# A four-layer float32 block: two mask levels of its recurrence copied by ScalarE, two small steps given to GpSimd, and the conditioning chunks spread anew

## The reference, cut to what matters

```python
for l in range(DEPTH):
    mod = silu_c @ w_ada[l] + b_ada[l]
    sh_a, sc_a, g_a, sh_f, sc_f, g_f = jnp.split(mod[:, None, :], 6, axis=-1)
    hx = rmsnorm(x) * (1 + sc_a) + sh_a
    ux = hx @ w_in[l]
    ...                       # Fourier mixer, attention, recurrence (below)
    x = x + g_a * (jnp.concatenate([fx, ax, rx], axis=-1) @ w_out[l])
    x = x + g_f * swiglu(rmsnorm(x) * (1 + sc_f) + sh_f, w_gate[l], w_up[l], w_down[l])

def hg_gate(z, lb):           # per direction d, columns OFF_Z + 256 d of u
    k = (1.0 - lb) * jax.nn.sigmoid(-z)
    log_f = jnp.log(lb + (1.0 - lb) * jax.nn.sigmoid(z))
def step(s, inp):             # a chunk of tokens, forwards and backwards
    cum = jnp.cumsum(lf, axis=2)
    s_new = exp(last) * s + einsum('bhsd,bhse->bhde', kc * exp(last - cum), vc)
    o_inter = einsum('bhtd,bhde->bhte', qc * exp(cum), s)
    att = einsum('bhtd,bhsd,bhtsd->bhts', qc, kc, exp(masked cum_t - cum_s))
    return s_new, o_inter + einsum('bhts,bhse->bhte', att, vc)
```

## Time and profile before

| | us |
|---|---|
| median of 3 runs (2050.8 to 2056.23) | 2055.1 |
| the profiled execution | 2060.7 |
| its span | 2058.5 |
| PE busy (x12110) | 1798.2 (87%) |
| DVE busy | 1325.0 (64%) |
| ACT busy | 825.8 (40%) |
| POOL busy | 60.2 (3%) |
| mean granted PE clock | 0.911 |

### The profile page before, as it was taken

One profiled execution on the slowest core, in us unless ns is written; L12 is line 12 of the kernel. 1 busy time (PEld: TensorE's weight loads), 2 busy tenths in 40 slices (PEclk: granted clock), 3 DMA queues, 4 the chain that ended last, 5 costly groups with the idle time before them and its releaser, 6 DMA issues.

```text
span 2058.5 us, 30617 instructions
## 1 busy us (share of the span) xinstructions
PE 1798.2 (87%) x12110; PEld 1615.2 (78%) x12110; DVE 1325.0 (64%) x2468; ACT 825.8 (40%) x1593; POOL 60.2 (3%) x133
## 2 busy tenths in 40 slices
PE   4799878989999999897787999777799996879997
PEld 2689667978888888796577998675799976769996
DVE  1435868558877565587665888657478875474544
ACT  3433743142312232436524343356344434554432
POOL 0000022000000000000110000000000000000000
PEclk8899988889999999898578999988899999899999
DMA  9462011145546653332216898631489853314653
GB/s 283 129 205 64 25 47 38 31 134 164 179 159 205 184 179 109 92 105 65 70 34 180 264 273 272 203 97 27 144 241 273 278 201 112 104 42 138 183 179 126
DMA packets 359116, 300.32 MB, mean 146 GB/s; under 512 B 8048, under 2 KB 333408, under 8 KB 358720
## 3 DMA queue, kind: packets, MB, share of 16 engines
q1 hardware_dynamic: 357584, 294.22, 46.4%
q0 software_dynamic: 1392, 4.15, 0.9%
HBM read 297.30 MB, written 1.05 MB: 145 GB/s over the span
## 4 chain that ended last, share of the span: by engine, by line
PE 72%; DVE 12%; DMA 6%; issue 5%; ACT 5%; SPq 0%; DVEq 0%; ACTq 0%; POOLq 0%
PE bank L862 69%; PE bank L876 3%; ACT whigh L1391 2%; DMA raw<-in_w_down 1%; DVE wlow L1821 1%; DMA raw<-in_w_up 1%; DVE A L2243 1%; DMA raw<-in_ffn_w_out 1%; DVE A L1918 1%; DVE A L2120 1%; DVE HTL L1924 1%; DVE ACC L1837 1%; DMA A<-in_w_ada 1%; DMA AWH<-in_ada_w 1%; ACT A L1566 1%
## 5 line engine op out<-in xcount | busy, mean ns | idle before, releaser
L1821 DVE TENSOR_TENSOR wlow<-raw,whigh 128x2048 fp32r<-128x2048 f32 (+1 forms) x183 | 410.0, 2243 | 335.8 <-ACT whigh L1391 335.6
L1391 ACT ACTIVATE whigh<-raw 128x2048 fp32r<-128x2048 f32 (+1 forms) x183 | 343.2, 1877 | 553.7 <-PE bank L862 335.3
L862 PE MATMUL bank<-HTH,whigh 128*128 128x256 f32 (+1 forms) x1424 | 449.1, 315 | 12.5 <-DVE HTL L1924 12.5
L862 PE MATMUL bank<-HTH,wlow 128*128 128x256 f32 (+1 forms) x1424 | 444.0, 312 | 0.0
L862 PE MATMUL bank<-HTL,whigh 128*128 128x256 f32 (+1 forms) x1424 | 443.9, 312 | 0.0
L862 PE MATMUL bank<-whigh,HTH 128*128 128x256 f32 (+1 forms) x1008 | 296.8, 294 | 20.4 <-DVE HTL L1924 8.4
L862 PEld LDWEIGHTS bank<-HTH,whigh 128*128 128x128 f32 x1424 | 277.8, 195 | 26.1 <-issue 13.6
L862 PE MATMUL bank<-wlow,HTH 128*128 128x256 f32 (+1 forms) x1008 | 292.7, 290 | 0.0
L862 PE MATMUL bank<-whigh,HTL 128*128 128x256 f32 (+1 forms) x1008 | 292.3, 290 | 0.0
L862 PEld LDWEIGHTS bank<-HTH,wlow 128*128 128x128 f32 x1424 | 277.3, 195 | 13.6
L862 PEld LDWEIGHTS bank<-HTL,whigh 128*128 128x128 f32 x1424 | 277.8, 195 | 12.6
(11 more groups left out here) (207 smaller groups left out, 2191.0 us busy)
## 6 DMA issues: line engine op xcount, KB each, us to landing
raw<-in_ffn_w_in SPq DMA_DIRECT2D x88, 512.0 KB, 5.2
A<-in_ada_w SPq DMA_DIRECT2D x42, 1024.0 KB, 7.3
A<-in_w_ada SPq DMA_DIRECT2D x32, 1024.0 KB, 5.4
raw<-in_w_gate SPq DMA_DIRECT2D x44, 512.0 KB, 5.2
raw<-in_w_up SPq DMA_DIRECT2D x44, 512.0 KB, 6.3
raw<-in_ffn_w_out SPq DMA_DIRECT2D x20, 1024.0 KB, 5.0
raw<-in_w_in SPq DMA_DIRECT2D x18, 1024.0 KB, 6.2
raw<-in_w_down SPq DMA_DIRECT2D x18, 1024.0 KB, 6.7
```

The source lines that it names most:

```text
L862: return nc.tensor.matmul(out, lhsT, rhs, start=start, stop=stop, skip_group_check=True)
L1391: nc.scalar.activation(parts(loads[n])[0], raw_slot(loads[n]), ACT.Copy).then_inc(*made("split_high", loads[n]))
L1821: V.tensor_tensor(low, raw_slot(loads[n]), as_float(high), ALU.subtract).then_inc(*made("split_low", loads[n]))
```

## The change

1. **Conditioning respread** (`ada_plan`): 31 chunks beside the feed-forward of layer 0 (30 before), 10 in the recurrence of layer 1 (6), 17 beside the feed-forward of layer 1 (20), 18 beside that of layer 2 (20). The ten spots of the recurrence are two after step 0, one after each of steps 1, 2 and 3, two after step 4, one after each of 5, 6 and 7; before they were one after each of steps 0, 1, 2, 4, 5 and 6.
2. **ACT's order in the feed-forward**: `late` (the drain of `mod`) before `split`.
3. **Two levels copied as blocks**: the levels are weighed and multiplied in the order 4, 5, 6, 0, 1, 2, 3. Levels 6 and 5 are copied by ACT in three copies (64 partitions x 256, and twice 32 x 128); DVE masks 4, 0, 1, 2, 3 after those copies.
4. **The clamp** is done by POOL in place, for each of 4 tiles once (128 x 512), ahead of `gained`; `gate_in` is gone, and ACT's `gates_open` reads `U`.
5. **`QP`** is made by POOL (`query_decays`), one step later in POOL's order than the step's own pairs.

```diff
@@ ada_plan
-    give(feed_forward(0, 30))
-    give(scan(1, 6))
-    give(feed_forward(1, 20))
+    give(feed_forward(0, 31))
+    give(scan(1, 10))
+    give(feed_forward(1, 17))
     give(feed_forward(2, len(chunks)))
@@
+        LEVEL_ORDER = (4, 5, 6, 0, 1, 2, 3)
+        MASK_ORDER = (4, 0, 1, 2, 3)
+        def block_copies(d):
+            out = []
+            for j in (6, 5):
+                w = 1 << j
+                for b in range(P // (2 * w)):
+                    keys, queries = (2 * w * b + w * i for i in (1 - later(d), later(d)))
+                    out.append((j, slice(keys, keys + w), slice(queries, queries + w), slice(w * b, w * b + w)))
+            return out
+        def need_masked(eng, l, s, j):
+            eng.wait_ge(*upto("masked", l, s, 4 if j == ROUND_END[1] else MASK_ORDER[-1]))
+            eng.wait_ge(*upto("blocks_copied", l, s))
@@ gpsimd
+            def clamped(l):
+                for t in tiles_of(l, "mix"):
+                    ...
+                    z = U[:, t, OFF_Z:OFF_Z + 512]
+                    nc.gpsimd.tensor_scalar(z, z, LOWEST_GATE, None, ALU.max).then_inc(*made("clamped", l, t))
+            def query_decays(l, s, t, before):
+                for p in range(2):
+                    pool.wait_ge(*drained("e", l, s, p, 1))
+                pool.wait_ge(*drained("qt2", l, t))
+                if before:
+                    pool.wait_ge(*upto("read_out", l, s - 2))
+                nc.gpsimd.tensor_tensor(QP[:, s % 2], HW[s % 2][:, :, 7, :], qt2(l, t), ALU.mult) \
+                    .then_inc(*made("query_decays", l, s))
@@ own_pairs, ahead of the pairs of output step n
+                    if n:
+                        query_decays(l, outs[n - 1], scan_steps(l)[outs[n - 1]][1], n - 1 >= 2)
@@ tensor
-                    pe.wait_ge(*upto("masked", l, s, LEVELS - 1))
+                    need_masked(pe, l, s, ROUND_END[0])
+                    pe.wait_ge(*upto("query_decays", l, s))
-                        for j in range(LEVELS):
+                        for j in LEVEL_ORDER:
@@ scalar, recurrence
-                    act.wait_ge(*upto("gate_in", l, s))
-                    if l and n >= 2:
-                        act.wait_ge(*upto("gates", l, s - 2))
-                    nc.scalar.activation(HE[g], HS[g], ACT.Exp, scale=-1.0).then_inc(*made("gate_exp", l, s))
+                    act.wait_ge(*upto("clamped", l, t))
+                    if n >= 2:
+                        act.wait_ge(*(upto("gates", l, s - 2) if l else upto("gate_sum", l, s - 2)))
+                    z = U[:, t, OFF_Z + 256 * d:OFF_Z + 256 * d + 256]
+                    nc.scalar.activation(HE[g], z, ACT.Exp, scale=-1.0).then_inc(*made("gate_exp", l, s))
+                def copy_blocks(n):
+                    s, t, d, has_out = steps[n]
+                    act.wait_ge(*upto("product", "a", l, s, ROUND_END[1]))
+                    ...
+                    for j, keys, queries, at in block_copies(d):
+                        last = nc.scalar.activation(AS[keys, d, :, queries], PAIRS[1][keys, :, j % 4, at], ACT.Copy)
+                    last.then_inc(*made("blocks_copied", l, s))
                     if n + 2 < len(steps):
                         gates_open(n + 2)
+                    if has_out:
+                        copy_blocks(n)
@@ scalar, feed_forward (the same swap in the loop over "dn")
+                        late(("gu", l, f), by=2)
                         split(index[("gu", l, f)] + HIGH)
-                        late(("gu", l, f), by=2)
@@ vector
-                def gate_in(n):
-                    ...
-                    V.tensor_scalar(HS[s % 2], U[:, t, OFF_Z + 256 * d:OFF_Z + 256 * d + 256], LOWEST_GATE, None, ALU.max) \
-                        .then_inc(*made("gate_in", l, s))
-                    V.tensor_tensor(HS[g], HS[g], HE[g] if l else LF[g], ALU.add).then_inc(*made("gate_sum", l, s))
+                    z = U[:, t, OFF_Z + 256 * d:OFF_Z + 256 * d + 256]
+                    V.tensor_tensor(HS[g], z, HE[g] if l else LF[g], ALU.add).then_inc(*made("gate_sum", l, s))
-                    V.tensor_tensor(QP[:, s % 2], hw[:, :, 7, :], qt2(l, t), ALU.mult)
-                    for j in range(LEVELS):
+                    for j in LEVEL_ORDER:
@@ mask
-                    for j in range(LEVELS):
+                    dve.wait_ge(*upto("blocks_copied", l, s))
+                    for i, j in enumerate(MASK_ORDER):
                         dve.wait_ge(*upto("product", "a", l, s, ROUND_END[j // 4]))
```

More of the change, by code:

```diff
@@ L760, in gained @@
                         .then_inc(*made("gained", l, t))
+            def clamped(l):
+                for t in tiles_of(l, "mix"):
+                    for j, (a, b) in enumerate(col_groups(l)):
+                        if OFF_Z <= a < OFF_I:
+                            pool.wait_ge(*drained("u", l, j, t))
+                    z = U[:, t, OFF_Z:OFF_Z + 512]
[8 more added lines that the diff above has]
+                    .then_inc(*made("query_decays", l, s))
             def own_pairs(l):
@@ L823, in _ @@
                     pool.dma_start(W4, io["w_four"][l].rearrange("(k p) c -> p k c", p=P)).then_inc(*made("four_in", l, by=16))
+                    clamped(l)
                     gained(l)
@@ L1211, in recurrence @@
                 modulation_end()
-                pe.wait_ge(*upto("masked", l, outs[-1], LEVELS - 1))
+                need_masked(pe, l, outs[-1], ROUND_END[0])
                 pe.wait_ge(*upto("scanned", l, outs[-1]))
@@ L1657, in take_decays @@
                         if n >= 2 and steps[n - 2][3]:
-                            act.wait_ge(*upto("weighed", l, s - 2, LEVELS - 1))
+                            act.wait_ge(*upto("weighed", l, s - 2, LEVEL_ORDER[-1]))
+                            act.wait_ge(*upto("query_decays", l, s - 2))
                         nc.scalar.activation(KT2[s % 2], ps[:, 0:256].rearrange("p (k c) -> p k c", k=2), ACT.Copy) \
@@ L1678, in take_tails @@
                             .then_inc(*made("drained_act", "sf", l, s))
+                def copy_blocks(n):
+                    s, t, d, has_out = steps[n]
+                    act.wait_ge(*upto("product", "a", l, s, ROUND_END[1]))
+                    act.wait_ge(*upto("cleared", l))
+                    if n >= 2 and steps[n - 2][3]:
+                        act.wait_ge(*upto("read_out", l, s - 2))
+                    for j, keys, queries, at in block_copies(d):
+                        last = nc.scalar.activation(AS[keys, d, :, queries], PAIRS[1][keys, :, j % 4, at], ACT.Copy)
+                    last.then_inc(*made("blocks_copied", l, s))
                 for n in range(2):
@@ L1748, in feed_forward @@
                             key = ("dn", l, half, h, c)
+                            late(key, by=2)
                             if key != last_down(l):
                                 split(index[key] + HIGH)
-                            late(key, by=2)
                 late(None)
@@ L2166, in recurrence @@
                 V.memset(ST[1], 0.0)
-                link(V.memset(AS, 0.0))
-                def gate_in(n):
-                    s, t, d, has_out = steps[n]
-                    need_u(l, t, OFF_Z + 256 * d, OFF_Z + 256 * d + 256)
-                    if n >= 2:
-                        dve.wait_ge(*upto("closed_gate", l, s - 2))
-                    V.tensor_scalar(HS[s % 2], U[:, t, OFF_Z + 256 * d:OFF_Z + 256 * d + 256], LOWEST_GATE, None, ALU.max) \
-                        .then_inc(*made("gate_in", l, s))
+                V.memset(AS, 0.0).then_inc(*made("cleared", l))
+                dve.wait_ge(*upto("cleared", l))
                 def gate_sum(n):
@@ L2220, in weigh @@
                     if n and steps[n - 1][3]:
-                        dve.wait_ge(*upto("product", "a", l, s - 1, ROUND_END[1]))
+                        dve.wait_ge(*upto("product", "a", l, s - 1, ROUND_END[0]))
                     if n >= 2 and steps[n - 2][3]:
@@ L2269, in recurrence @@
                 for n in range(2):
-                    gate_in(n)
                     gate_sum(n)
@@ L2275, in recurrence @@
                         weigh(n)
-                    if n + 2 < len(steps):
-                        gate_in(n + 2)
                     if s < 6:
```

9 lines of the change are left out of this document (6 added, 3 removed).

## The result

The changed kernel took 2030.4 us (median of 3, 2028.6 to 2034.0) beside 2055.1: ratio 0.9889 [0.9857, 0.9921]. Timed again on another occasion (6 runs) it gave 0.9908 [0.9877, 0.9940]. So the gain is 19 to 23 us where 10.4 were forecast. The profiled execution took 2028.6 us, its span 2026.8.

A forecast was written before the change was run, and what follows sets the result against it. The prediction took TensorE to bound the kernel, with waits in the feed-forwards of layers 1 and 2 and layer 1's recurrence. Terms -26.1 + 17 - 0.8 - 1.5 + 1 = -10.4 gave 2044.7 us from 2055.1; range 2034 to 2058.

The forecast's parts named there:

- Part 1: Feed-forwards, mainly layers 1 and 2: ACT's swap and fewer chunks remove PE's waits and narrow matmuls, -26.1 us.
- the rival "slower": Feed-forwards: SP's chunk loads waiting for DVE's sums set the pace, so stages give little; 2062 us, chance 0.12.
- Part 2: Recurrence of layer 1: ten serial chunks in one buffer delay PE, +17 us, bounds +10 to +22.
- The +6.0 up to the levels of step 4: Recurrence of layer 1: chunks after the early steps make `prepare(5)` and the levels of step 4 later by 6.0 us.
- +7.7 for `prepare(6)`: Recurrence of layer 1: two chunks after step 4, the second waiting for its load, delay `prepare(6)` by 7.7 us.
- +3.0 for the clock: Recurrence of layer 1: a further stand of PE keeps step 5 at the slow clock, +3.0 us.
- Part 3: Masks in the recurrences: block copies gain 0.35 us a step at high clock, lose at low clock; -0.8 us in all.
- Part 4: Clamp and `QP` on POOL: earlier start in layer 0, -1.5 us; POOL and DVE contention, +1 us.
- the cheap recurrence: Rival: feed-forwards give 29 us, clock rises at once, ten chunks cost 11; 2036 us, chance 0.20.
- Weights take half the place: Rival: late weights replace part of PE's drain waits, feed-forwards of layers 1 and 2 give 8 us each; 2053 us, chance 0.23.

The follow-up runs named there:

- issue_later: Kernel before, with only the load of a chunk beside a feed-forward issued one weight tile later in SP's order; ratio 0.9863.
- spread_only: Kernel before, with only the plan of chunks changed, to 31/10/17/18; ratio 0.9949.
- swap_and_spread: Kernel before, with ACT's new order and the new plan of chunks, none of the recurrence's edits; ratio 0.9953.
- swap_only: Kernel before, with only ACT's order in the feed-forwards changed, plan 30/6/20/20 kept; ratio 0.9996.
- half_bytes: Kernel before, with chunks beside the feed-forwards of layers 1 and 2 loading half their bytes, all eight sums kept; ratio 0.9871.
- clamp_only: Kernel before, with the clamp alone moved to GpSimd and QP still made by DVE; ratio 0.9961.
- gates_only: Kernel before, with the clamp and the query decays on GpSimd; levels, masks and plan as before; ratio 0.9968.
- after_again: The changed kernel itself, timed and profiled once more beside the partial ones; ratio 0.9908 to the kernel before.

## Why the prediction was wrong, point by point

- **What bounds it: TensorE, and two places.** Right. Both places gave the gain or took it.
- **Part 1, -26.1.** The size was right, -24.5 where -26.5 was forecast for the two stages (mean of two profiles of the changed kernel, 397.8 for the sum of the two stages, against 422.3 over six kernels with the old plan). The cause was wrong, so the size was in part luck. I put it on the order on ACT; the swap gives nothing by itself or on top of the respread, and two or three chunks fewer do it all. The row that I read as proof, a small drain behind a `split` that waits 8.55 us for a DMA, showed the end of a chain whose start was SP's stand. I had that chain in the text, and in the rival "slower", but let fewer bytes cure it at DMA's rate instead of asking how long SP stood. My argument from DMA being near its limit, 0.94 busy in 25 us, fell too: `issue_later` has it 0.96 busy over 100 us, and PE waits for nothing. Its window 1120:1220 (DVE busy, then clock, DMA share, GB/s):

```profile
1120.00:1220.00 100.00, 85.08 (x128) 1.00 0.96 266
```

- **Part 2, +17: the step that failed.** The recurrence of layer 1 came out at -0.3 in the profile the result was read from and +7.7 in the next, 97.7 - 92.8 = +4.9 against the means: 12 us less than forecast, where the whole sum was off by 8 to 12. The waits stood where they were forecast, 15.2 us in all against 5.8 before. The +6.0 up to the levels of step 4 was near: from the memset to them it is 48.0 and 50.2 us in the two profiles of the changed kernel, and 43.6 to 45.4, mean 44.6, in the six with six chunks and without the edits: +4.5. What failed is the rest, +7.7 for `prepare(6)` and +3.0 for the clock: behind those levels only 0.4 came. The ten chunks by themselves (`spread_only`, `swap_and_spread`) cost 6.2 up to there and 2.2 behind, 8.4 in all. I had counted the +7.7 behind a level group of 6.24 us. In `spread_only` and in the changed kernel that group takes 3.34 us, so the chunk behind it is done sooner, the second load goes out sooner, and `prepare(6)` starts 13.3 us after the start of the levels, not 17.8 (10.1 before). From the levels of step 5 to the end the two kernels without the edits take 31 and 32 us, where those with six chunks take 33 or more. The clock had the wrong sign. What raised it isn't shown: three of the six kernels with six chunks have the group of step 4 at 3.34 us as well (`swap_only`, `half_bytes`, `issue_later`). And the edits, put at about nothing in layer 1 but for 1.7 at the start, gave 3.5 us at ten chunks and 8.2 at six.
- **Part 3, masks, -0.8.** The working in a step was right (masks end 6.0 us after the levels; 5.9 forecast). Two slow level groups in layer 0 were to lose 1.3. That of step 7 did lose 0.9 (from its levels to the last add 11.8 us for 10.9); that of step 6 became 4.5 us long where before it took 5.3, and from it to the next group it is 10.0 us for 10.7. With part 4 layer 0 gave 4.9 us and not 1.3 (-0.8 - 1.5 + 1).
- **Part 4.** The start as forecast (exp at 263.49 right after ACT's drain; 264.68 before). Missed: in the short steps of layer 1 the clamp is part of the chain, 1.1 us up to the fourth exp; little of that is left at step 4. Some 4 us of the gates' share in layer 1 lie after step 4, where I said that they give nothing in a step, and their cause is open. As to contention, the estimate from the Trainium skill's rule (SBUF — State Buffer, section SBUF: two separate sides: the loser of the shared port pair waits for the whole instruction) allowed 8 us for `QP` on GpSimd. `clamp_only` without that move stands at 0.9961 [0.9942, 0.9980], `gates_only` with it at 0.9968 [0.9945, 0.9991]: neither its cost nor its gain is seen. Such a wait does occur: one clamp of layer 1 took 3.44 us for 1.48, beside a DVE operation of 2.31 (last section).
- **Not in the prediction at all:** the 31st chunk at the end of layer 0, "0.4 us on PE", put 3.4 us into the gap. I counted its work and not where its drain stands in ACT's order.
- **The sum.** -4.9 (recurrence 0) - 1.2 (to the first SiLU, 80.5 against 81.7) + 3.4 + 4.9 - 24.5 = -22.3, within what the two timings say (-22.8 and -18.9). The stages are from one profile each; added up for the edits alone or the respread alone they come to 13 to 14 us each, where the times say 10. The measured 2030.4 lies below the range, which ended at 2034 because the cheap recurrence was priced with chunks at 11 and edits at -2.3.
- **The rivals.** "Slower through SP" named the true mechanism, but its point (stages under 17 together) was not reached with 17 and 18 chunks. "Weights take half the place" is what `swap_only` shows: with twenty chunks the weights take all of it.

## What to carry to other kernels

A wait of the bound engine on something tiny can be the end of a chain: follow it through the issuing queue, and list that queue's own waits, before naming a cause. In a queue that issues in order, a load that may wait belongs behind the loads that are ready; here its place in the order gave 28 us, a buffer more gave nothing, and half the bytes or half the arithmetic gave no more than the place did (26.5 and 25.3). Count a moved piece of work at the place where its last small step lands, and read a chain stage by stage: what hides in long steps can be the chain of the short ones.

## What the runs showed of the hardware that was not expected

- Two profiles of one kernel differ by 8 us in one recurrence. The last level group took 3.34 us (2.4 GHz) in one and 6.24 us (1.2 GHz) in the other, and from it to the end it is 7.7 and 11.9 us; the granted clock in 1050:1075 was 0.93 and 0.64.
- With half the sums left out DMA brought 269 GB/s over 200 us, with twenty chunks and no wait of PE for weights; a share of 0.94 in one window before had not been a limit.
- A GpSimd clamp of 128 x 512 took 1.47 to 1.51 us in the attentions, but for one: that at 932.84 in layer 1 took 3.44 us. It started inside a DVE operation with two inputs from SBUF that ended at 934.94, and it is longer than the others by 2.0 us, nearly what was left of that operation (2.1). In `after_again`, `gates_only` and `clamp_only` the same clamp starts inside the same DVE operation and takes 3.44 us. The eight clamps (duration in ns, least, median, most) and that operation, in the changed kernel:

```profile
L786 POOL TENSOR_SCALAR A<-A x8: 1475/1492/3443, 204.8 to 937.7; 128x512 f32<-128x512 f32 x8
932.63 2.31 DVE L1877 TENSOR_TENSOR wlow<-raw,whigh 128x2048 fp32r<-128x2048 f32 x1 [4.09 <-ACT whigh L1432]
```

- The other way round, a DVE product of 128 x 128 beside a GpSimd product of 256 columns took up to 0.82 us, where the median of those alone is 0.28.
